# Low parts of the wide groups' weights moved from GpSimd to VectorE, eight PSUM banks in those groups, and two seams reordered

## The chip, the cores and the metric

One core of a Trainium2 chip runs the whole program. The metric is device time of one execution in microseconds (us), the median of the runs; lower is better. TensorE (PE in the rows) runs the matrix multiplies, VectorE (DVE), ScalarE (ACT) and GpSimd (POOL) the elementwise work, and the sync engine's queue (SP) issues most DMAs.

## The reference

A two-layer model steps over 1024 prompt rows, 16 meta rows and 8 x 16 decode rows: an mLSTM layer, then a sliding-window attention layer, each followed by the same kind of feed-forward block. Only the two feed-forward blocks matter here:

```python
def swiglu(x, w_gu, w_dn):
    g, u = jnp.split(x @ w_gu, 2, axis=-1)
    return (jax.nn.silu(g) * u) @ w_dn
...
h = h + swiglu(rmsnorm(h, norm_ffn[l]), w_gate_up[l], w_down[l])
```

`w_gu` is 1024 x 5632 and `w_dn` 2816 x 1024, all float32. The first block runs on 1168 rows of tokens, the second on 1152.

## The kernel before

The class `Ffn` is one feed-forward block; it is used twice. Every float32 operand is split into a high part (ScalarE's copy to the fp32r type, `product_hi`, L415) and a low part (the operand minus its high part, `product_lo`, L426), and a product is three matmuls: high x high, high x low, low x high.

A block has three stages. First four plain column blocks of gate and up (L835 to L848). Then 20 **wide groups** g = 0 to 19: each makes two column blocks of gate (g even) or up (g odd) by Strassen's scheme in Winograd's form, seven products i = 0 to 6 instead of eight. A product (`wide_product`, L723) is 24 matmuls of 292 (second block: 288) columns with four 128-row weight tiles. Products are numbered p = 7g + i. Then 10 **down groups** (g = 20 to 29) do the same for `w_dn` (`down_product`, L750), where a product has two halves nn of 12 matmuls. Below, the **entry** is wide group 0 and what leads to it, and the **down seam** is the step from group 19 to group 20.

Nothing is scheduled by a tool: every engine has its own order, written out by hand, and semaphores between engines. Around a product p these are the steps:

- SP loads four weight quarters of 128 x 512 for each group (`load_quarter`, L308). Quarters A11 and A21 of the next group wait for low parts i = 2 and 3 of this group, A12 for i = 5 and A22 for i = 6.
- Four sums of quarters (`weight_sum` n = 0 to 3, L432) make the weights of products 2 to 5: GpSimd does them for group 0, VectorE for all others (`weight_sums`, L1066).
- ScalarE makes the high part of product p + 2 after product p - 1 is done (L423, L676); GpSimd then makes its low part at once (L492 to L516). Weights sit in a ring of three.
- TensorE waits for the low part of p and for the eviction of p - 2 (L727 to L731); the products alternate between two pairs of PSUM banks.
- VectorE, in order: the eviction of p (`wide_out`, L919), then sums of weights, then forms of the hidden rows (`form_sum`, L976). In an odd group the evictions of products 1, 4 and 5 are three operations in a row: add from PSUM (L950), scale (L953), multiply with the gate (L961).

At the entry VectorE also makes the operands t2, t3 and t4 of the products and their low parts (`t_low`, L900). At the down seam the forms of the hidden rows come back from DRAM (`load_hidden`, L326), ScalarE makes their high parts (L616), and the low parts (`hidden_low`, L467) are VectorE's, but for forms 1 and 3, which are GpSimd's (L496, L501).

Of the kernel before, what the change touches and what calls it, by code (L numbers as in the profile page):

```python
# [139 lines left out]
class Ffn:  # L140


    def __init__(self, nc, a, s, name, layer, gain, parity, base, early, tok, before, turns=None):
# [45 lines left out]
        self.t_raw, self.t_scaled, self.t4_lo = share["t_raw"], share["t_scaled"], share["t4_lo"]  # L189
# [7 lines left out]
        counts = dict(w_hi=4 + 210 + 2, w_lo=8 + 210 + 4, w_sum=4 * 30, x_hi=40, x_lo=38, x_sq=24, x_sum=21, t_raw=16, t_scaled=8,  # L197
                      t4_lo=4, total=3, root=3, rst=3, gu_done=12 + 140 + 140, gu_evac=12 + 140 + 140, silu=46, hid=46,
                      g_scaled=30, u_scaled=30, hid_hi=41, hid_lo=39, hid_sum=40, dn_done=self.n_down, dn_evac=self.n_down)
# [153 lines left out]
    def sync(self, sp, last=None):  # L353
# [10 lines left out]
        for g in range(WIDE_GROUPS + DOWN_GROUPS):  # L364
            for i in range(N_PRODUCTS):
# [49 lines left out]
    def product_hi(self, act, p):  # L415
# [7 lines left out]
        act.wait_ge(self.gu_done, self.done_at(p - 3))  # L423
# [34 lines left out]
    def t_low_pool(self, pool, k):  # L458

        hi, lo = self.wide_x(6, k)  # L460
        if k == 2:
            for x in range(4):
                pool.wait_ge(self.hid_st[x], self.z["hid_st"][x] + 16)
        pool.wait_ge(self.x_hi, self.z["x_hi"] + 36 + k - 1)
        pool.tensor_tensor(lo, self.wide_raw(6, k), hi.bitcast(F32), ALU.subtract).then_inc(self.t4_lo, 1)

    def hidden_low(self, eng, kk, j, done):  # L467

        m = 7 * kk + j
        hi, lo = self.combo(m)  # L470
        eng.wait_ge(self.hid_hi, self.z["hid_hi"] + m + 1)
        eng.tensor_tensor(lo, self.hidden_raw(m), hi.bitcast(F32), ALU.subtract).then_inc(done, 1)

# [12 lines left out]
    def gpsimd(self, pool):  # L486
# [5 lines left out]
        for g in range(WIDE_GROUPS + DOWN_GROUPS):  # L492
            p = 7 * g
            self.product_lo(pool, p)
            if g == WIDE_GROUPS:
                self.hidden_low(pool, 0, 1, self.t4_lo)  # L496
            if g == 0:
# [2747 lines left out]
```

## Time and profile before

| | us |
|---|---|
| median of 3 runs | 2460.42 (2460.22 to 2460.51) |
| the profiled execution | 2460.95 |
| its span, first to last instruction | 2459.2 |
| TensorE busy | 2410.8 (98%) |
| VectorE busy | 1673.7 (68%) |
| GpSimd busy | 990.4 (40%) |
| ScalarE busy | 865.4 (35%) |
| mean granted clock of TensorE | 0.995 |

Busy time is the time in which an engine ran an instruction of the program; idle time of an engine that is not the bottleneck costs nothing. A window of the trace is given from its start to its end in us of the span. PEclk is the share of full speed that TensorE's clock was granted.

### The profile page before, as it was taken

What the parts mean: (1) busy time and instruction counts of PE and PEld (TensorE: products, weight loads), DVE (VectorE), ACT (ScalarE), POOL (GpSimd) and SP (SyncE); (2) the same over time, 40 slices, a digit from 0 to 9 for tenths busy, and PEclk for the clock granted to TensorE, in tenths of its full rate; (3) what the DMA queues carried; (4) which work ended last, traced back from release to release, by engine and by line L of the source; (5) the groups of instructions that cost most, each with busy time, mean ns of one, the idle gap of its engine ahead of it and who ended that gap; (6) DMA issues with size and microseconds to landing.
All of it is one profiled execution on the core that took longest, in us unless ns stands there. A gap on an engine that the chain in (4) does not pass through costs nothing. (4 is left out here: it accounts for less than half of the span.)

```text
span 2459.2 us, 42910 instructions
## 1 busy us (share of the span) xinstructions
PE 2410.8 (98%) x16730; PEld 2340.1 (95%) x16730; DVE 1673.7 (68%) x2540; ACT 865.4 (35%) x1765; POOL 990.4 (40%) x818
## 2 busy tenths in 40 slices
PE   9999999999999999999999999999999999999997
PEld 8989999999999999999999989889999999999996
DVE  6445454439767667697879656757877776788775
ACT  5223232326222222243425556436322222243334
POOL 1222222422544444444447344335544444444542
PEclk9999999999999999999999999999999999999999
DMA  4445565211222223264522234210132332254423
GB/s 160 144 131 146 166 179 181 71 36 38 86 87 98 91 92 101 84 208 141 165 87 59 46 81 104 57 35 27 64 106 72 97 108 90 97 193 148 135 87 122
DMA packets 303533, 259.50 MB, mean 106 GB/s; under 512 B 52856, under 2 KB 261164, under 8 KB 303300
## 3 DMA queue, kind: packets, MB, share of 16 engines
q1 hardware_dynamic: 303140, 256.70, 34.1%
q8 instruction: 135, 2.21, 0.4%
q14 instruction: 66, 0.54, 0.1%
q10 hardware_dynamic: 192, 0.04, 0.0%
HBM read 180.95 MB, written 77.54 MB: 105 GB/s over the span
## 5 line engine op out<-in xcount | busy, mean ns | idle before, releaser
L430 POOL TENSOR_TENSOR wh<-raw,wh 128x512 fp32r<-128x512 f32 x360 | 525.9, 1461 | 645.0 <-ACT wh L424 644.7
L424 ACT ACTIVATE wh<-raw 128x512 fp32r<-128x512 f32 x360 | 227.3, 631 | 700.8 <-PE psum L746 261.4
L746 PE MATMUL psum<-xh,wh 128*128 128x292 f32 (+1 forms) x2560 | 460.3, 296 | 7.1 <-DVE ffn_gate_quarters L941 6.6
L746 PEld LDWEIGHTS psum<-xh,wh 128*128 128x128 f32 x2560 | 383.7, 189 | 7.7 <-issue 7.7
L746 PE MATMUL psum<-xl,wh 128*128 128x292 f32 (+1 forms) x1280 | 276.6, 298 | 0.0
L2781 PE MATMUL psum<-xh,wh 128*128 128x384 f32 (+1 forms) x792 | 274.6, 347 | 1.3 <-DVE fr_tmp L2971 0.5
L2781 PE MATMUL psum<-xl,wh 128*128 128x384 f32 (+1 forms) x792 | 270.0, 341 | 0.0
L2781 PE MATMUL psum<-xh,wl 128*128 128x384 f32 (+1 forms) x792 | 268.8, 339 | 0.0
L974 DVE TENSOR_TENSOR h<-h,psum 128x584 f32<-128x584 f32 (+1 forms) x280 | 205.1, 752 | 83.2 <-PE psum L771 82.9
L771 PE MATMUL psum<-ffn_slot,wh 128*128 128x292 f32 (+1 forms) x1536 | 212.5, 300 | 9.7 <-DVE ffn_part L946 9.7
L771 PEld LDWEIGHTS psum<-ffn_slot,wh 128*128 128x128 f32 x1536 | 210.2, 192 | 10.3 <-issue 10.3
L746 PEld LDWEIGHTS psum<-xl,wh 128*128 128x128 f32 x1280 | 206.4, 189 | 0.0
L2781 PEld LDWEIGHTS psum<-xh,wh 128*128 128x128 f32 x792 | 148.8, 188 | 3.9 <-DVE xl L2941 1.1
L2781 PEld LDWEIGHTS psum<-xh,wl 128*128 128x128 f32 x792 | 149.1, 188 | 0.1
L2781 PEld LDWEIGHTS psum<-xl,wh 128*128 128x128 f32 x792 | 148.9, 188 | 0.1
L2654 POOL TENSOR_TENSOR wl<-raw,wh 128x512 fp32r<-128x512 f32 x62 | 82.6, 1353 | 138.3 <-ACT wh L2467 138.3
L771 PE MATMUL psum<-xh,wh 128*128 128x292 f32 (+1 forms) x960 | 130.9, 296 | 0.0
L771 PEld LDWEIGHTS psum<-xh,wh 128*128 128x128 f32 x960 | 128.7, 188 | 0.0
L430 POOL TENSOR_TENSOR wh<-ffn_w_extra,wh 128x512 fp32r<-128x512 f32 x60 | 84.3, 1406 | 95.4 <-ACT wh L424 95.4
L746 PE MATMUL psum<-ffn_t2h,wh 128*128 128x292 f32 (+1 forms) x640 | 117.6, 295 | 2.8 <-issue 2.8
L746 PE MATMUL psum<-ffn_t1h,wh 128*128 128x292 f32 (+1 forms) x640 | 117.5, 295 | 1.9 <-POOL wh L430 1.9
L771 PE MATMUL psum<-xl,wh 128*128 128x292 f32 (+1 forms) x864 | 118.8, 296 | 0.0
(330 smaller groups left out, 5128.1 us busy)
## 6 DMA issues: line engine op xcount, KB each, us to landing
raw<-in_w_gate_up SPq DMA_DIRECT2D x160, 256.0 KB, 3.5
raw<-in_w_down SPq DMA_DIRECT2D x80, 256.0 KB, 3.1
ffn_form_d<-ffn_gate_quarters SPq DMA_DIRECT2D x50, 292.0 KB, 2.2
ffn_form_d<-ffn_gate_quarters SPq DMA_DIRECT2D x50, 288.0 KB, 2.2
raw<-in_a_w_in SPq DMA_DIRECT2D x24, 512.0 KB, 4.8
ffn_slot_raw<-ffn_form_d SPq DMA_DIRECT2D x16, 584.0 KB, 5.0
fr_qkv<-qkv_d SPq DMA_DIRECT2D x36, 256.0 KB, 3.8
ffn_slot_raw<-ffn_form_d SPq DMA_DIRECT2D x16, 576.0 KB, 5.2
```

The lines of the kernel that those rows point to most:

```text
L424: act.activation(self.ring(p)[0], self.quarter(b), ACT.Copy).then_inc(self.w_hi, 1)
L430: pool.tensor_tensor(lo, self.quarter(WEIGHT_OF[p % 7]), hi.bitcast(F32), ALU.subtract).then_inc(self.w_lo, 1)
L746: y = pe.matmul(psum[:, bank + c, 0:N], w[:, k, :], x[:, N * c:N * c + N], start=(FRESH[i] and k == 0 and m == 0), stop=(k == 3 and m == 2 ...
L771: y = pe.matmul(psum[:, bank + c, 0:N], w[:, k, cols], x[:, k, N * c:N * c + N], start=(FRESH[i] and k == 0 and m == 0), stop=(k == 1 and ...
L974: dve.tensor_tensor(x, x, psum[:, bank:bank + 2, 0:N], ALU.add).then_inc(self.gu_evac, 1)
L2654: pool.tensor_tensor(wl[:, slot_of(n), v], raw[:, n % 2, v], wh[:, slot_of(n), v].bitcast(F32), ALU.subtract).then_inc(w_lo, 1)
L2781: mm_ = pe.matmul(psum[:, g % DB, 0:nt], w[:, k, :], x[:, k, t0:t0 + nt], start=(k == 0 and m == 0), stop=(k == KD - 1 and m == 2))
```

## The change

In the wide groups, low parts of the weights from p = 9 to p = 139 are made by VectorE, right behind the eviction of p - 2; GpSimd keeps p = 0 to 8 and the down groups. The products of even groups use banks 0, 1, 4, 5 and those of odd groups 2, 3, 6, 7, so the first two products of a group wait for no eviction of the group before. At the entry ScalarE makes the high parts of products 0 and 1 earlier, GpSimd does all four sums right after low parts 0 and 1, and two low parts of operand t4 go from GpSimd to VectorE. At the down seam three sums of group 20 go from VectorE to GpSimd, ahead of its low part 141; two hidden low parts go from GpSimd to VectorE; the hidden forms are loaded in another order; and the first down product waits half by half for older evictions.

```diff
+    def wide_bank(self, g, i):
+        return 2 * (g % 2) + 4 * (i % 2)
...
     def sync(self, sp, last=None):
                     if i == 2:
                         self.load_quarter(sp, g + 1, A11)
                         self.load_quarter(sp, g + 1, A21)
+                    if g == 19 and i in (3, 4):
+                        for j in ((0, 1), (2,))[i - 3]:
+                            self.load_hidden(sp, 0, j)
                     if i == 4:
                         self.load_quarter(sp, g + 1, A12)
                     if i == 5:
                         self.load_quarter(sp, g + 1, A22)
-                if g == 19 and i >= 3:
-                    for j in ((0, 1), (2, 3), (4, 5), (6,))[i - 3]:
+                if g == 19 and i >= 5:
+                    for j in ((3,), (4, 5, 6))[i - 5]:
                         self.load_hidden(sp, 0, j)
...
     def product_hi(self, act, p):
-        act.wait_ge(self.gu_done, self.done_at(p - 3))
+        act.wait_ge(self.gu_done, self.done_at(p - 3) if p > 1 else self.z["gu_done"] + 8 + p)
...
     def gpsimd(self, pool):
-        for g in range(WIDE_GROUPS + DOWN_GROUPS):
-            p = 7 * g
+        for p in range(7 * (WIDE_GROUPS + DOWN_GROUPS)):
+            if 9 <= p < 140:
+                continue
+            if p == 140:
+                self.weight_sum(pool, WIDE_GROUPS, 0)
+                pool.wait_ge(self.w_lo, self.lo_at(139))
             self.product_lo(pool, p)
...
+            if p < 2:
+                self.weight_sum(pool, 0, p)
+            if p == 1:
+                self.weight_sum(pool, 0, 2)
+                self.weight_sum(pool, 0, 3)
+            if p == 7 * WIDE_GROUPS:
+                self.weight_sum(pool, WIDE_GROUPS, 1)
+                self.weight_sum(pool, WIDE_GROUPS, 2)
...
     def scalar(self, act, x_free, h_ready):
         gate_part(0)
-        for k in (2, 3, 0, 1):
-            t2_hi(k)
+        t2_hi(2)
+        t2_hi(3)
+        self.product_hi(act, 0)
+        self.product_hi(act, 1)
+        t2_hi(0)
+        t2_hi(1)
         gate_part(1)
         t3_scale(0)
         t3_scale(1)
-        self.product_hi(act, 0)
-        self.product_hi(act, 1)
...
         def wide_product(g, i):
-            bank = 4 * ((g + i) % 2)
+            bank = self.wide_bank(g, i)
             pe.wait_ge(self.w_lo, self.lo_at(p))
             if p < 2:
                 pe.wait_ge(self.gu_evac, self.z["gu_evac"] + (8, 12)[p])
+            elif g == 1 and i < 2:
+                pe.wait_ge(self.root, self.z["root"] + 3)
+            elif i < 2:
+                pe.wait_ge(self.gu_evac, self.evac_at(7 * (g - 2) + 6 - i))
             else:
                 pe.wait_ge(self.gu_evac, self.evac_at(p - 2))
...
         def down_product(g, i):
-                pe.wait_ge(self.gu_evac, self.evac_at(p - 2, nn))
+                if p == 140:
+                    pe.wait_ge(self.gu_evac, self.evac_at(7 * (18 + nn) + 6))
+                else:
+                    pe.wait_ge(self.gu_evac, self.evac_at(p - 2, nn))
...
         def weight_sums(g, i):
-            if i in (4, 5, 6) and g + 1 < WIDE_GROUPS + DOWN_GROUPS:
+            if i in (4, 5, 6) and g + 1 < WIDE_GROUPS + DOWN_GROUPS and g + 1 != WIDE_GROUPS:
                 self.weight_sum(dve, g + 1, i - 4)
...
                 wide_out(g, i)
...
+                if 9 <= 7 * g + i + 2 < 140:
+                    if 7 * g + i + 2 == 9:
+                        dve.wait_ge(self.w_lo, self.lo_at(8))
+                    self.product_lo(dve, 7 * g + i + 2)
                 weight_sums(g, i)
...
+                if g == 0 and i == 2:
+                    for x in range(4):
+                        dve.wait_ge(self.hid_st[x], self.z["hid_st"][x] + 16)
+                    t_low(6, 2, 37)
+                    t_low(6, 3, 38)
...
                 if g == 19 and i in (4, 6):
-                    hidden_lo(0, i // 2 - 2 if i == 4 else 2)
+                    for j in ((0, 1), (), (2,))[i - 4]:
+                        hidden_lo(0, j)
...
                 down_out(g, i)
                 weight_sums(g, i)
+                if g == WIDE_GROUPS and i == 0:
+                    hidden_lo(0, 3)
```

## Rows read from the trace of the kernel before

**Rows 1.** The page, part 1: busy us (share of the span) xinstructions.

```profile
PE 2410.8 (98%) x16730; PEld 2340.1 (95%) x16730; DVE 1673.7 (68%) x2540; ACT 865.4 (35%) x1765; POOL 990.4 (40%) x818
```

**Rows 2.** Windows: us; busy of PE, PEld, DVE, ACT, POOL (instructions); PEclk; DMA share; GB/s.

```profile
600.43:631.69 31.26, 24.97 (x170) 24.12 (x169) 30.36 (x28) 12.09 (x20) 19.34 (x13) 0.95 0.15 46
721.90:1015.09 293.19, 293.19 (x2186) 293.19 (x2185) 206.33 (x233) 73.57 (x117) 125.60 (x91) 1.00 0.29 92
1060.20:1090.54 30.34, 25.42 (x170) 25.21 (x169) 30.27 (x28) 14.28 (x16) 17.04 (x10) 0.89 0.77 252
1731.62:1761.43 29.81, 24.31 (x169) 23.67 (x169) 28.97 (x28) 12.39 (x20) 18.03 (x12) 0.94 0.16 48
1805.86:2139.06 333.20, 333.20 (x2523) 333.20 (x2522) 235.52 (x269) 84.93 (x134) 151.12 (x105) 1.00 0.29 94
2183.67:2213.38 29.71, 24.97 (x168) 24.76 (x169) 29.64 (x28) 14.16 (x16) 16.82 (x10) 0.89 0.77 260
```

**Rows 3.** Waits of TensorE: who waited for whom, us in total, times, longest.

```profile
PE psum L746 <- DVE ffn_gate_quarters L941: 6.6, 2, 3.3
PE psum L746 <- POOL wh L430: 1.9, 2, 0.9
```

**Rows 4.** Windows inside the first entry, columns as in rows 2.

```profile
606.80:610.20 3.40, 1.84 (x14) 1.64 (x13) 3.40 (x3) 0.00 (x0) 2.87 (x2) 1.00 0.00 0
617.20:620.20 3.00, 0.00 (x0) 0.00 (x0) 3.00 (x3) 0.69 (x1) 3.00 (x3) 1.00 0.45 135
620.40:623.60 3.20, 3.08 (x13) 3.11 (x14) 3.20 (x4) 1.21 (x2) 3.06 (x3) 0.50 0.03 7
```

**Rows 5.** Timeline of VectorE, wide group 9: start us, us, engine line op.

```profile
828.43 0.77 DVE L950 TENSOR_TENSOR ffn_part<-psum,ffn_part 128x584 f32<-128x584 f32 x1 [2.46 <-PE psum L746]
829.23 1.89 DVE L953 TENSOR_TENSOR ffn_part<-ffn_part,rstd 128x584 f32<-128x584 f32 x1
831.15 0.77 DVE L961 TENSOR_TENSOR ffn_gate_quarters<-ffn_gate_quarters,ffn_part 128x584 f32<-128x584 f32 x1
831.84 0.69 DVE L443 TENSOR_TENSOR ffn_w_extra<-raw 128x512 f32<-128x512 f32 x1
```

**Rows 6.** Timeline of GpSimd, wide group 9.

```profile
829.20 1.30 POOL L430 TENSOR_TENSOR wh<-raw,wh 128x512 fp32r<-128x512 f32 x1 [1.95 <-ACT wh L424]
```

**Rows 7.** The page, part 6: DMA issues xcount, KB each, us to landing.

```profile
raw<-in_w_gate_up SPq DMA_DIRECT2D x160, 256.0 KB, 3.5
```

**Rows 8.** Timeline of VectorE, first entry.

```profile
592.05 1.44 DVE L903 TENSOR_TENSOR ffn_t2l<-ffn_t_raw,ffn_t2h 128x584 fp32r<-128x584 f32 x2
...
612.42 3.63 DVE L903 TENSOR_TENSOR xl<-ffn_part,xh 128x584 fp32r<-128x584 f32 x2
...
619.66 1.43 DVE L941 COPY ffn_gate_quarters<-psum 128x584 f32<-128x584 f32 x2
```

**Rows 9.** Windows of VectorE alone: us, busy, clock, DMA share, GB/s.

```profile
592.00:620.40 28.40, 28.26 (x30) 1.00 0.15 53
1054.00:1106.00 52.00, 51.83 (x53) 0.93 0.65 217
```

**Rows 10.** Window of GpSimd alone, first entry.

```profile
592.00:620.40 28.40, 18.40 (x11) 1.00 0.15 53
```

**Rows 11.** Timeline of TensorE, first down seam.

```profile
1068.56 12.51 PE L771 MATMUL psum<-ffn_slot,wh 128*128 128x292 f32 x72 [4.92 <-DVE ffn_part L946]
```

**Rows 12.** Timeline of VectorE, first down seam.

```profile
1053.96 0.77 DVE L950 TENSOR_TENSOR ffn_part<-psum,ffn_part 128x584 f32<-128x584 f32 x1 [2.46 <-PE psum L746]
...
1057.97 1.37 DVE L472 TENSOR_TENSOR ffn_slot<-ffn_slot_raw,ffn_slot 128x1168 fp32r<-128x1168 f32 x1
...
1067.66 0.75 DVE L946 TENSOR_TENSOR ffn_part<-psum,rstd 128x584 f32<-128x584 f32 x1
...
1105.13 1.42 DVE L974 TENSOR_TENSOR h<-h,psum 128x584 f32<-128x584 f32 x2
```

**Rows 13.** Timeline of ScalarE, first down seam.

```profile
1058.33 1.19 ACT L616 ACTIVATE ffn_slot<-ffn_slot_raw 128x1168 fp32r<-128x1168 f32 x1 [0.65 <-DMA ffn_slot_raw<-ffn_form_d]
```

More of the change, by code:

```diff
@@ L456, in weight_sum @@
         x.then_inc(self.w_sum, 1)
[L458 to L472, printed above, removed]
     def last_lo(self, eng, j, half):
@@ L598, in t4_hi @@
             if k < 2:
-                act.wait_ge(self.t4_lo, self.z["t4_lo"] + k + 1)
+                act.wait_ge(self.x_lo, self.z["x_lo"] + 36 + k + 1)
             act.activation(self.wide_x(6, k)[0], self.wide_raw(6, k), ACT.Copy).then_inc(self.x_hi, 1)
@@ L738, in wide_product @@
             if g == 0 and i == 6:
-                pe.wait_ge(self.t4_lo, self.z["t4_lo"] + 2)
-                pe.wait_ge(self.x_lo, self.z["x_lo"] + 38)
+                pe.wait_ge(self.x_lo, self.z["x_lo"] + 40)
             hi, lo = (w.rearrange("p (k n) -> p k n", k=4) for w in self.ring(p))
@@ L755, in down_product @@
             if sub == 0:
-                if kk == 0 and i in (1, 3):
-                    pe.wait_ge(self.t4_lo, self.z["t4_lo"] + (3 if i == 1 else 4))
-                elif kk == 0:
-                    pe.wait_ge(self.hid_lo, self.z["hid_lo"] + (1, 1, 2, 2, 3, 4, 5)[i])
-                else:
-                    pe.wait_ge(self.hid_lo, self.z["hid_lo"] + 7 * kk + i - 1)
+                pe.wait_ge(self.hid_lo, self.z["hid_lo"] + 7 * kk + i + 1)
             hi, lo = (w.rearrange("p (k n) -> p k n", k=2) for w in self.ring(p))
@@ L792, in down_blocks @@
                 if t % 3 == 0:
-                    pe.wait_ge(self.hid_lo, self.z["hid_lo"] + 33 + 2 * (t // 3 + 1))
+                    pe.wait_ge(self.hid_lo, self.z["hid_lo"] + 35 + 2 * (t // 3 + 1))
                 if t < 2:
@@ L818, in down @@
             for c, (t0, nt) in enumerate(tok):
-                pe.wait_ge(self.hid_lo, self.z["hid_lo"] + 33 + 2 * (c + 1))
+                pe.wait_ge(self.hid_lo, self.z["hid_lo"] + 35 + 2 * (c + 1))
                 for m in range(KD):
@@ L922, in wide_out @@
             pair, up = g // 2 + 1, g % 2
-            bank = 4 * ((g + i) % 2)
+            bank = self.wide_bank(g, i)
             x = psum[:, bank:bank + 2, 0:N]
@@ L996, in hidden_lo @@
         def hidden_lo(kk, j):
-            self.hidden_low(dve, kk, j, self.hid_lo)
+            m = 7 * kk + j
+            hi, lo = self.combo(m)
+            dve.wait_ge(self.hid_hi, self.z["hid_hi"] + m + 1)
+            dve.tensor_tensor(lo, self.hidden_raw(m), hi.bitcast(F32), ALU.subtract).then_inc(self.hid_lo, 1)
         def last_hidden_lo(c):
@@ L2236, in front @@
     started = {x: [0, 0] if x == "w_loaded" else 0 for x in s["share"]}
-    again = dict(w_sum=(ncd, HA), t4_lo=(nco, HA), t_raw=(den, 10 * HA), t_scaled=(hsd, 10 * HA), g_scaled=(ssq, 10 * HA),
+    again = dict(w_sum=(ncd, HA), t_raw=(den, 10 * HA), t_scaled=(hsd, 10 * HA), g_scaled=(ssq, 10 * HA),
                  u_scaled=(msd, 10 * HA), hid_sum=(rden, 10 * HA))
```

30 lines of the change are left out of this document (4 added, 26 removed).

## The prediction

> **What bounds the kernel now.** I read the busy shares first: TensorE is busy 98% of the span [rows 1], so all idle time of it together is 48 us. Then I looked where that time lies, with windows cut at the starts of groups [rows 2]. In the stretch 721.90 to 1015.09 of the first block (13 wide groups, 91 products) TensorE is busy 293.19 of 293.19 us, one product each 3.222 us; in the second block 333.20 of 333.20 us for 105 products, 3.173 each. Nothing waits there, so faster low parts and more banks have nothing to gain in those groups. The time is lost at four seams: the entries last 31.26 and 29.81 us against 22.55 and 22.21 for a steady group, the first down groups, with as many matmuls, 30.34 and 29.71 [rows 2]. That is 8.7 + 7.6 + 7.8 + 7.5 = 31.6 us, the ceiling of any gain.
>
> The waits of TensorE say who ends these losses: VectorE's evictions L941 and the low parts of GpSimd [rows 3]; at the first down seam 4.92 us for the eviction L946 [rows 11]. Part of the loss is the clock. In the entry TensorE did nothing from 617.20 to 620.20, and the granted clock was then 0.5, that is 1.2 GHz, from 620.40 to 623.60 while it was busy; a stop of about 1.5 us at 606.80 to 610.20 left it at 1.0, that is 2.4 GHz [rows 4]. Last I asked why VectorE is late, and the answer is that it is saturated: 28.26 of 28.40 us before the entry's worst stop, and 51.83 of 52.00 us across the down seam [rows 9].
>
> **How VectorE and GpSimd meet.** Two low parts of 128 x 584 take 1.44 us on VectorE alone and 3.63 us beside a busy GpSimd; two evictions of the same size from PSUM take 1.43 us, GpSimd busy or not [rows 8]. So an operation with both inputs in SBUF that meets one of GpSimd pays (3.63 - 1.44) / 2 = 1.1 us, and one that reads PSUM pays nothing. In wide group 9 the scaling L953 took 1.89 us while GpSimd's low part ran at 829.20; the multiply after it, of the same shape, 0.77 us [rows 5, 6].
>
> **Part 1, the low parts on VectorE in the wide groups.** Without GpSimd there, no operation of VectorE pays the 1.1 us. But the low part now stands in VectorE's order, behind the eviction. I lay out the second half of an odd group with free durations [rows 5]: add, scale and multiply start 0.80 us apart, and the low part 0.69 after the multiply, so 2.29 us from the first start; it takes 0.69 (the sum L443 has its size and its two SBUF inputs) and ends at 2.98. The sum behind product 4 starts at 2.89, and product 5's chain at 3.49, since back-to-back operations overlap by 0.09; its low part, which product 0 of the next group needs, ends at 3.49 + 2.98 = 6.47. Group 9 starts at 721.90 + 4 x 22.553 = 812.11, its product 5 at 828.22, the next group at 834.66. VectorE starts on product 4 at 828.43, so the low part ends at 834.90. From the end of an eviction, 1067.66 + 0.75, to TensorE's start at 1068.56 are 0.15 us [rows 11, 12]; I take 0.1 of them as the signal. TensorE starts 0.34 us late. Behind product 1 of an odd group the low part ends 0.21 + 2.98 + 0.1 = 3.29 us after a product's start, 0.07 late. Even groups have two operations at most and recover. Nine of the ten odd groups precede a wide group: 9 x 0.34 + 10 x 0.07 = 3.8 us. In the second block two periods are 0.10 us shorter and VectorE's operations some 0.07: 9 x 0.37 + 10 x 0.08 = 4.1. **Toll: +8 us.** Bounds: 5 us if the signal costs nothing, 20 if each of the three long evictions of an odd group stops TensorE by 0.35.
>
> What else hangs on this order: quarter A22 of the next group is issued once low part i = 6 is made, now behind the eviction of product 4 instead of about 4 us earlier on GpSimd. Its sum is wanted behind product 5, at 6.38 us in the layout above; 2.98 + 3.5 us [rows 7] is 6.48, so VectorE may stand 0.1 us there. Behind that stand the eviction of product 6 and low part 1 of the next group, which has 0.5 us to spare. I cost it at nothing; a load 0.6 us slower than the median would show. A12 is issued one eviction earlier and lands in time. The banks are costed at nothing too: no eviction ends a wait in the steady stretch, neither before nor in this layout.
>
> **Part 2, the entry.** VectorE stays the bound, so I count what it meets up to the eviction that releases product 4 (619.66 before, [rows 8]). Its list of operations up to there is the same; the two t4 low parts come behind it. Before, GpSimd runs eleven operations from 592 to 620.4 [rows 10], the last of them, a t4 low part, at its end; of the ten others about one falls beside PSUM reads, so they cost it some 9.8 us. Now high parts 0 and 1 come some 3 us earlier, as soon as their quarters land, and low parts 0 and 1 and all four sums run in one train of six from about 592 to 602.5, each against an operation with two SBUF inputs; low parts 2 to 5 meet four more. Ten meetings are 11 us, and where VectorE reaches an operation just after GpSimd has begun it pays up to 1.2: 11.3. So product 4 starts 1.5 us later than at 620.5. The waits move forward: product 1 now waits some 3 us for the last up eviction (L881), 2 about 1.9, 3 about 0.8, 4 about 2.5. Against that, the 3.08 us of matmuls at 1.2 GHz [rows 4] cost 1.5 us before, and with shorter stops I take the clock as full. Net 0 in the first block, +0.4 in the second, where VectorE had been idle ahead of the train. Bounds for each block: -4.4 (four meetings fewer) to +3 (the clock falls again, and one meeting more).
>
> **Part 3, the down seam.** VectorE begins at 1053.96 [rows 12]. Three eviction operations and low part 139 end at 1056.95. GpSimd's low part 140 waits for that and holds VectorE to 1058.2; two hidden low parts of 1.28 us each (row at 1057.97, less the overlap) follow to 1060.75, their high parts being there by 1059.5 [rows 13, 12]. Product 138's chain, with two meetings with GpSimd's sums, ends at 1064.6, and the eviction of 139 at 1065.4, where it was 1068.41. TensorE's product 140 starts at 1060.2, but its second half now waits for that eviction: 3.6 us. Product 141 then starts at 1067.1 instead of 1068.56. VectorE goes on with hidden low parts 2, 3 and 4 and two evictions; product 143 waits 1.5 us for the eviction of 141 at 1074.9. That is 5.2 us lost for 7.8 before, **-2.6 us**, and -2.4 in the second block.
> Why not more: VectorE has no pause up to 1106 [rows 9]. Its addition for product 150 (first half) ends at 1105.88 [rows 12], and product 152, which needs it, starts at 1090.54 + 5 x 3.222 = 1106.65: a slack of 0.8. What TensorE wins earlier it gives back there, but for what VectorE itself wins: about 2 us, as it makes 0.6 + 2.6 us more, three sums of 0.6 less, and meets GpSimd for some 6 us instead of 9.4. Bounds: -7.8 (seam gone) to +3 for each block.
> On SP the hidden forms 0 to 2 go ahead of A12, which now waits for low part 138; A12 lands about 1 us later, covered by GpSimd's two sums ahead of low part 141.
>
> **Sum.** 2460.95 (the profiled execution: span 2459.2 and 1.75 around it) + 8 + 0.4 - 5.0 = 2464.35. That execution is 0.53 above the median, so **2464**. A measurement of this kernel can tell 0.2%, 4.9 us: the band of no change is 2455.5 to 2465.3. My own range for this case, 2459 to 2470, crosses its upper end. Chance 0.54, of which 0.34 inside the band and 0.20 above.
>
> The steady toll is a short stop of TensorE about every 22 us, a stop of 0.3 us, and a stop of 1.5 us left the clock at 2.4 GHz [rows 4]. The Trainium skill, page "TensorE: Matmul & The Clock Gate", section "A second HAM failure mode: psum-queue depth-cycling", speaks against this change: it says that small idle gaps between groups of matmuls can by themselves make the clock swing between its two levels. By that rule the sum would be the fourth rival below.
>
> **The rivals.**
> *Slower, by the seam.* The hidden low parts 0 and 1 now stand ahead of two evictions on VectorE, and wait for forms that come over DMA. For it: DMA engines are busy 0.77 of the first down group [rows 2], and ScalarE waited for the second form until 1058.33 [rows 13]. Each us by which its high part comes after 1059.5 goes through to the eviction of 139. If it comes as late as 1061.7, product 141 starts at 1069.2, the clock falls as before, and the seam costs 0.6 us more than before instead of 2.5 less: +6.2 for both, 2471. Against it: the first three forms are issued earlier than before. It decides from about 1061 on. Chance 0.18.
> *Faster, VectorE freed.* If GpSimd's early train meets PSUM reads and pauses, four meetings fewer give -4.4 us at each entry, and the seams another 1.5: 2464 - 8.8 - 3 = 2452. For it: the train comes before VectorE's longest run of SBUF operations. Against it: VectorE has no pause from 592 on [rows 9], and only some six of its operations up to product 4 read PSUM. Chance 0.22.
> *No toll.* The change may not lengthen VectorE's order as I lay it out, if the long evictions run shorter than their free rows: 2456. Against it: 0.77 us stands in every such row. Chance 0.04.
> *Clock.* If each of the 20 odd groups' stops brings 3.2 us at half speed, 1.6 us lost each [rows 4], 32 us are added: 2496. Against it are the stop of 1.5 us that left the clock alone [rows 4] and the clock of 1.0 in the steady stretches, where nothing stops [rows 2]. Chance 0.02.
>
> **How the numbers follow.** Faster 0.22; the same 0.34 + 0.04 = 0.38; slower 0.20 + 0.18 + 0.02 = 0.40. The range goes from 2452, the faster case, to 2475, above the seam's case and with a toll of some 16 us: outside lie half of the faster case, the clock and a tail, under 0.2.
>
> **What would show it.** Right: in the odd groups TensorE waits some 0.3 us for VectorE's L430 at the start of the next group, and VectorE's L953 takes 0.77 everywhere; the entries stay near 31 us with the longest waits on L881, L941; product 140 stops between its halves. Wrong: no idle TensorE in wide groups 1 to 19 (no toll), entries of 27 us or less, a down seam under 24 us, or a granted clock of 0.5 inside the steady stretch.

## The result, and the profile after

The changed kernel takes **2466.76 us** (median of 9 runs, 2464.96 to 2469.66); the kernel before, beside it on the same chip, 2460.22 (9 runs, 2459.48 to 2463.93). The ratio is 1.0027 with a 95% interval of 1.0019 to 1.0035: slower by 6.5 us. 2464 was forecast, with a range of 2452 to 2475. The profiled execution of after has a span of 2464.2 us, 5.0 longer than the one before.

The page, part 1, of after (busy us, share of the span, instructions), which answers to [rows 1]:

```profile
PE 2416.2 (98%) x16730; PEld 2337.1 (95%) x16730; DVE 1714.0 (70%) x2804; ACT 869.8 (35%) x1765; POOL 611.2 (25%) x554
```

GpSimd has lost 379 us of work, and VectorE has gained only 40, though it makes 262 of the low parts: most of what they cost it saves on meetings.

Windows of after, cut at the starts of its groups as [rows 2] (columns as there): in each block the entry, the wide groups 1 to 19, the first and the second down group.

```profile
600.65:630.43 29.78, 25.07 (x170) 24.22 (x169) 29.38 (x33) 12.08 (x20) 13.05 (x9) 0.94 0.16 49
630.43:1063.63 433.20, 433.19 (x3194) 429.54 (x3193) 321.99 (x470) 112.33 (x173) 2.59 (x2) 1.00 0.30 96
1063.63:1091.17 27.54, 23.01 (x170) 22.57 (x169) 26.75 (x27) 14.07 (x17) 15.31 (x10) 1.00 0.78 262
1091.17:1117.24 26.07, 23.33 (x170) 22.65 (x169) 24.11 (x28) 7.95 (x11) 11.50 (x8) 1.00 0.41 134
1735.37:1764.60 29.23, 23.16 (x169) 22.32 (x169) 28.84 (x34) 11.95 (x20) 10.82 (x7) 1.00 0.18 57
1764.60:2191.22 426.62, 426.54 (x3195) 422.64 (x3193) 319.75 (x470) 112.10 (x173) 2.63 (x2) 1.00 0.30 96
2191.22:2218.83 27.61, 23.97 (x171) 23.74 (x169) 27.51 (x29) 14.22 (x17) 14.29 (x10) 0.94 0.80 271
2218.83:2241.02 22.19, 22.19 (x171) 22.19 (x170) 19.98 (x27) 7.60 (x10) 10.61 (x7) 1.00 0.46 148
```

From the same cuts in both traces: the wide groups took 428.51 and 422.24 us before, so they lose 4.7 and 4.4. The entries win 1.5 and 0.6, the first down groups 2.8 and 2.1. The second down group of the first block, 22.49 before, now takes 26.07 and gives 3.6 back. With 0.7 won elsewhere that is the 5.0 of the spans.

PE counts as busy in nearly the whole wide stretch, and its list of waits has nothing there. The weight loads (PEld) have lost 3.7 and 4.0 us of it (429.54 of 433.20, 422.64 of 426.62; before, 428.50 of 428.51 and 422.01 of 422.24), and their own list of waits names VectorE's low part L436, 18 times:

```profile
PEld psum L731 <- DVE wh L436: 4.2, 18, 0.2
```

How it comes about shows where VectorE's list is laid beside the start of the next group (timelines of VectorE and of TensorE, wide group 9 of after, columns as in [rows 5]):

```profile
832.76 0.76 DVE L933 TENSOR_TENSOR ffn_part<-psum,ffn_part 128x584 f32<-128x584 f32 x1
833.55 0.77 DVE L936 TENSOR_TENSOR ffn_part<-ffn_part,rstd 128x584 f32<-128x584 f32 x1
834.35 0.77 DVE L944 TENSOR_TENSOR ffn_gate_quarters<-ffn_gate_quarters,ffn_part 128x584 f32<-128x584 f32 x1
835.04 0.68 DVE L436 TENSOR_TENSOR wh<-raw,wh 128x512 fp32r<-128x512 f32 x1
```

```profile
835.36 0.43 PE L731 MATMUL psum<-ffn_t4h,wh 128*128 128x292 f32 x2
835.78 0.54 PE L731 MATMUL psum<-xh,wh 128*128 128x292 f32 x2
```

Matmuls start every 0.134 us, so the next pair was due at 835.63; the low part (L436) ends at 835.72 and TensorE goes on at 835.78, a stop of 0.15 us. The first pair behind it takes 0.54 us instead of 0.43, another 0.11. This second price is also paid where TensorE does not stop at all. At product 3 of the odd group the low part ends at 822.47, in time for the matmul due at 822.52. But elsewhere the load of a matmul's weights starts 0.13 us ahead of it, during the matmul before, and here load and matmul start together (loads and matmuls at product 3, of after, then of lo_ahead, an experiment below in which no product of these groups waits):

```profile
822.52 0.19 PEld L731 LDWEIGHTS psum<-ffn_t1h,wh 128*128 128x128 f32 x1
822.52 0.40 PE L731 MATMUL psum<-ffn_t1h,wh 128*128 128x292 f32 x1
```

```profile
820.47 0.19 PEld L731 LDWEIGHTS psum<-ffn_t1h,wh 128*128 128x128 f32 x1
820.60 0.29 PE L731 MATMUL psum<-ffn_t1h,wh 128*128 128x292 f32 x1
```

The trace of before shows this price as well, behind a stop in its first entry:

```profile
613.70 0.54 PE L746 MATMUL psum<-ffn_t1h,wh 128*128 128x292 f32 x2 [0.93 <-POOL wh L430]
614.07 0.43 PE L746 MATMUL psum<-ffn_t1l,wh 128*128 128x292 f32 x2
```

In after it is paid at product 6 too (832.30, its low part ready at 832.24). So a pair of groups loses 0.48 us: 0.11 in product 3 (3.32 us instead of 3.22), 0.11 in product 6 and the stop of 0.15 behind it (3.48 together), and 0.11 in product 0 of the next group (3.34). In each block that is nine stops, 1.3 and 1.5 us in all, and 29 such starts, 3.1 us. Where 0.26 us is called a stop in the expectations below, that is the 0.11 of product 6 and the stop of 0.15 behind it. L953 (L936 in after), which took 1.89 us before [rows 5], takes 0.77.

Waits of TensorE in after, in place of [rows 3]:

```profile
PE psum L754 <- DVE ffn_part L929: 7.2, 2, 3.6
PE psum L731 <- DVE ffn_gate_quarters L924: 4.2, 2, 2.1
PE psum L731 <- DVE ffn_up L864: 3.8, 2, 2.0
PE psum L754 <- DVE h L957: 3.7, 4, 1.6
```

The first is the stop between the halves of product 140: only the first half of it waits for an older eviction than before (132), the second for a newer one (139; in the kernel before it was 138). The next two are products 4 and 1 of the entries. Of the last, three are new, in the second down group of the first block; the fourth, 0.9 us, is product 143.

### The profile page after: what moved, and what is told of

Read it like the earlier page. It is cut to its first block and busy times, and to the rows that moved or that the text cites. A ratio compares the mean times of both kernels' runs of the same rounds, so it can differ in the third digit from the quotient of the medians.

```text
span 2464.2 us, 42912 instructions
## 1 busy us (share of the span) xinstructions
PE 2416.2 (98%) x16730; PEld 2337.1 (95%) x16730; DVE 1714.0 (70%) x2804; ACT 869.8 (35%) x1765; POOL 611.2 (25%) x554
## 5 line engine op out<-in xcount | busy, mean ns | idle before, releaser
L731 PE MATMUL psum<-xl,wh 128*128 128x292 f32 (+1 forms) x1280 | 276.0, 297 | 0.0
L436 POOL TENSOR_TENSOR wh<-raw,wh 128x512 fp32r<-128x512 f32 x136 | 208.4, 1534 | 242.8 <-ACT wh L430 235.3
L449 POOL TENSOR_TENSOR ffn_w_extra<-raw 128x512 f32<-128x512 f32 x4 | 6.1, 1523 | 845.0 <-DMA raw<-in_w_down 845.0
L436 DVE TENSOR_TENSOR wh<-raw,wh 128x512 fp32r<-128x512 f32 x224 | 152.8, 682 | 0.0
L731 PE MATMUL psum<-ffn_t4h,wh 128*128 128x292 f32 (+1 forms) x640 | 120.1, 299 | 0.0
```

The costliest lines, as they stand in the source:

```text
L436: pool.tensor_tensor(lo, self.quarter(WEIGHT_OF[p % 7]), hi.bitcast(F32), ALU.subtract).then_inc(self.w_lo, 1)
L449: x = pool.tensor_tensor(q(EXTRA), q(A11), q(A21), ALU.subtract)
L731: y = pe.matmul(psum[:, bank + c, 0:N], w[:, k, :], x[:, N * c:N * c + N], start=(FRESH[i] and k == 0 and m == 0), stop=(k == 3 and m == 2 ...
```

## The experiments

The table has the medians, the ratio to before with its interval, and the stages of each profiled execution, cut at the starts of groups as above (us; first block / second block). The kernels ran on several chips; each ratio is to before on the same chip, and there before took 2460.0 to 2460.5.

| kernel | median | ratio (95%) | entry | wide 1-19 | 1st down group | 2nd down group |
|---|---|---|---|---|---|---|
| before | 2460.22 | 1 | 31.26 / 29.81 | 428.51 / 422.24 | 30.34 / 29.71 | 22.49 / 22.18 |
| after | 2466.76 | 1.0027 (1.0019-1.0035) | 29.78 / 29.23 | 433.20 / 426.62 | 27.54 / 27.61 | 26.07 / 22.19 |
| lo_gpsimd | 2457.99 | 0.9993 (0.9984-1.0002) | 29.78 / 30.75 | 428.52 / 422.05 | 26.47 / 26.85 | 22.49 / 22.18 |
| lo_only | 2470.70 | 1.0047 (1.0034-1.0060) | 31.35 / 29.92 | 433.78 / 427.48 | 29.92 / 28.54 | 22.49 / 22.19 |
| old_banks | 2467.13 | 1.0030 (1.0019-1.0042) | 30.37 / 30.74 | 434.46 / 428.06 | 26.00 / 25.38 | 22.69 / 26.03 |
| lo_ahead | 2453.84 | 0.9978 (0.9969-0.9987) | 29.77 / 31.17 | 428.51 / 422.05 | 26.67 / 26.23 | 22.49 / 24.76 |
| before_lo_ahead | 2460.22 | 1.0000 (0.9991-1.0009) | 31.37 / 28.47 | 428.51 / 424.39 | 28.80 / 26.29 | 25.04 / 24.75 |
| seam_undone | 2473.89 | 1.0057 (1.0045-1.0070) | 31.30 / 30.72 | 433.47 / 427.34 | 31.55 / 30.84 | 22.49 / 22.18 |
| entry_undone | 2465.20 | 1.0024 (1.0015-1.0033) | 32.30 / 30.02 | 433.31 / 427.64 | 28.85 / 26.47 | 22.49 / 26.16 |
| sums_late | 2454.07 | 0.9977 (0.9968-0.9986) | 31.91 / 30.63 | 428.51 / 422.05 | 26.83 / 28.01 | 22.49 / 22.19 |
| seam_form_later | 2453.19 | 0.9973 (0.9963-0.9983) | 29.76 / 30.75 | 428.51 / 422.05 | 27.00 / 26.67 | 22.49 / 22.19 |
| best_old_entry | 2454.61 | 0.9977 (0.9968-0.9986) | 31.38 / 29.96 | 428.51 / 422.05 | 26.95 / 26.68 | 22.49 / 22.19 |
| entry_vector | 2443.81 | 0.9933 (0.9920-0.9945) | 25.87 / 24.87 | 428.51 / 422.05 | 27.30 / 26.63 | 22.49 / 22.19 |
| low141_first | 2444.55 | 0.9935 (0.9921-0.9949) | 25.87 / 24.81 | 428.51 / 422.05 | 27.04 / 27.90 | 22.65 / 22.19 |

### Where the toll comes from: lo_gpsimd, lo_only, old_banks, lo_ahead, before_lo_ahead

**lo_gpsimd**: the changed kernel, low parts back on GpSimd.

```diff
-            if 9 <= p < 140:
-                continue
...
-                pool.wait_ge(self.w_lo, self.lo_at(139))
...
-                if 9 <= 7 * g + i + 2 < 140:
-                    if 7 * g + i + 2 == 9:
-                        dve.wait_ge(self.w_lo, self.lo_at(8))
-                    self.product_lo(dve, 7 * g + i + 2)
```

> The changed kernel, with the low parts of the wide groups back on GpSimd; the eight banks, the entry and the down seam stay as changed. Theory (the toll is the place of the low parts in VectorE's order): the 0.26 us stop ahead of the product that follows each odd group, and the two slow restarts with it, go; wide groups 1 to 19 take 428.5 and 422.2 us again instead of 433.2 and 426.6, 9.1 us less, and the time is near 2457.5 us if entry and seam stay as they are. Rival 1 (the toll is the eight banks, whose owners are waited for): nothing changes, 2466. Rival 2 (what VectorE is spared beside an idle GpSimd pays at the down seam): the toll goes, but the low parts 133 to 139 meet VectorE's work there, and up to 3 us per block come back, 2459 to 2463.

2457.99 us, 8.8 less than after, and the wide groups are back at 428.52 and 422.05. Banks, entry and seam were left in, so the toll is the low parts' alone. (The profiled execution, at 2452.77, is the lowest of eleven; the steady wide groups are the safest thing to read in it.) Rival 2 is not seen: the first down groups are not longer than after's, and the median is that of the theory. The kernel is also all of the change but its main part, and is 2.1 us below the 2460.08 of before beside it, with an interval that does not exclude no change at all.

**lo_only**: the kernel before, with the lines that lo_gpsimd takes out put in, and nothing else.

> The kernel before, with only the low parts 9 to 139 of the wide groups moved to VectorE; four banks at a time, entry and down seam as before. Theory (place in VectorE's order): the toll alone, 9 us, and at the seams nothing or a little, 2467 to 2471 us; TensorE stops some 0.26 us behind each odd group. Rival 1 (the banks cause the toll): 2460, no stop. Rival 2 (freeing VectorE of GpSimd is worth more than the toll at the seam): 2464.

2470.70 us, at the upper end of the theory: the toll without the gains.

**old_banks**: the changed kernel, with

```diff
-        return 2 * (g % 2) + 4 * (i % 2)
+        return 4 * ((g + i) % 2)
...
-            elif i < 2:
-                pe.wait_ge(self.gu_evac, self.evac_at(7 * (g - 2) + 6 - i))
...
-                if p == 140:
-                    pe.wait_ge(self.gu_evac, self.evac_at(7 * (18 + nn) + 6))
-                else:
-                    pe.wait_ge(self.gu_evac, self.evac_at(p - 2, nn))
+                pe.wait_ge(self.gu_evac, self.evac_at(p - 2, nn))
```

> The changed kernel with the bank pairs of the kernel before: two pairs in turn, and each product waits for the eviction of the second one before it. Theory: the banks cost and gain nothing in the wide groups, so 2465 to 2468 us with the same stop of 0.26 us behind the odd groups; at the down seam the first half of product 140 then waits for the eviction of 138 and no longer for that of 139 between its halves. Rival (the eight banks cause the toll): 2457.5. Second rival (the banks hide a part of the toll): 2470 or more, with longer stops in the odd groups.

2467.13 us, the same as after. The longer wide stretch (by 1.3 and 1.4) is mostly the wait for the eviction of 138, which now comes ahead of product 140; the first down groups are shorter by 1.5 and 2.2. No effect of the eight banks on the time could be measured.

**lo_ahead**: the changed kernel with the same operations in another order.

```diff
         for i in range(N_PRODUCTS):
+            if 9 <= 7 * g + i + 2 < 140:
+                if 7 * g + i + 2 == 9:
+                    dve.wait_ge(self.w_lo, self.lo_at(8))
+                self.product_lo(dve, 7 * g + i + 2)
             wide_out(g, i)
...
-            if 9 <= 7 * g + i + 2 < 140:
-                if 7 * g + i + 2 == 9:
-                    dve.wait_ge(self.w_lo, self.lo_at(8))
-                self.product_lo(dve, 7 * g + i + 2)
             weight_sums(g, i)
```

> The changed kernel with one edit: VectorE makes the low part of product p + 2 ahead of its evicting operations for product p instead of behind them. All operations stay, only their order on VectorE changes. Theory (place in the order): VectorE is busy some 34 of 45 us in a pair of wide groups, so it has room; the low part is then made one product earlier, no product waits for it, wide groups 1 to 19 take 428.5 and 422.2 us and the time is near 2457.5 us, or below if the earlier quarter loads help the down seam. Rival 1 (VectorE has too much to do in an odd group, whatever the order): the stop stays or moves to an eviction, 2464 to 2468. Rival 2 (the eight banks): 2466.

2453.84 us: 12.9 less than after, and faster than before. Windows of the wide stretches, and the timeline of VectorE in the same odd group:

```profile
630.49:1059.00 428.51, 428.51 (x3194) 428.51 (x3193) 322.47 (x471) 112.88 (x174) 3.51 (x3) 1.00 0.30 98
1757.53:2179.58 422.05, 422.05 (x3194) 422.05 (x3193) 320.24 (x471) 112.49 (x173) 4.21 (x3) 1.00 0.31 99
```

```profile
829.52 0.69 DVE L449 TENSOR_TENSOR ffn_w_extra<-raw 128x512 f32<-128x512 f32 x1
830.12 0.68 DVE L436 TENSOR_TENSOR wh<-raw,wh 128x512 fp32r<-128x512 f32 x1
830.73 0.76 DVE L933 TENSOR_TENSOR ffn_part<-psum,ffn_part 128x584 f32<-128x584 f32 x1
```

The low part now stands ahead of the chain of its product (L933, L936, L944), is made 3.0 us earlier against the group's start (19.2 us into it, where after has 22.2), and nothing waits for it. VectorE's work is the same 322 us in the stretch: it was the place, not the amount. In the profiled executions, whose spans differ by 10.0 us, the wide groups give 9.3 and the first down groups 2.3: product 140 stops 2.3 us between its halves instead of 3.6.

**before_lo_ahead**: the kernel before, with low parts on VectorE in this order.

> The kernel before with only the low parts 9 to 139 moved to VectorE, each ahead of the evicting operations instead of behind them; banks, entry and down seam as before. Theory (the low parts ahead cost nothing and by themselves gain nothing in the wide groups, where nothing waited): no stop in the wide groups, 428.5 and 422.2 us; the first down groups 29 to 30 and 28 to 29 us; 2458 to 2460.5 us. Rival (a VectorE without GpSimd beside it reaches the down seam earlier and needs no reordered seam): first down groups under 27 us, 2454.

2460.22 us, the kernel before to within the interval. Well placed, the low parts on VectorE cost nothing and gain nothing. Its first down groups are shorter (28.80, 26.29), but both second ones give 2.6 back, and the end of the second wide stretch loses 2.3.

### The seam: seam_undone, sums_late, seam_form_later

**seam_undone**: the changed kernel with the parts of the diff at groups 19 and 20 taken back (sums on VectorE, hidden low parts 1 and 3 on GpSimd, SP's old order).

> The changed kernel with the down seam of the kernel before: VectorE makes the sums of the first down group, GpSimd the hidden low parts 1 and 3, and SP issues the hidden forms in the old order; low parts on VectorE, eight banks and the entry stay as changed. Theory (the seam as changed takes about 5 us off the two first down groups, and gives up to 3.6 us back in the second down group of a block): the first down groups take about 29.9 and 28.6 us, as in the run with the low parts alone on VectorE, instead of 27.5 and 27.6, and the second ones 22.5 and 22.2, so the time is 2466.5 to 2470 us. Rival (the seam won nothing that stays): 2464 to 2466.5.

2473.89 us, 7.1 more than after and beyond the theory. First down groups 31.55 and 30.84: the seam is worth 4.0 + 3.2 there, less the 3.6 that it gives back later. The waits of TensorE say why it is worse than lo_only's: with eight banks the second half of product 140 waits for the eviction of 139 (6.6 us), where in lo_only both halves ran before that wait (4.6 us, ahead of product 141).

```profile
PE psum L763 <- DVE ffn_part L938: 13.1, 2, 6.6
```

In this execution the entries, which it left alone, are 1.5 us longer each than in that of after; that is most of the rest. In both of these entries the granted clock fell behind product 4.

**sums_late**: lo_ahead, with the last pair's form sums and their stores in group 23.

```diff
-                if g == WIDE_GROUPS + 1 and i < 4:
+                if g == WIDE_GROUPS + 3 and i < 4:
                     form_sum(10, i)
```

It was made for the second down group. There, in after, the timeline of VectorE reads:

```profile
1091.97 0.69 DVE L454 TENSOR_TENSOR raw<-raw,ffn_w_extra 128x512 f32<-128x512 f32 x1 [1.49 <-DMA raw<-in_w_down]
...
1099.73 1.85 DVE L966 TENSOR_TENSOR ffn_part<-ffn_gate_quarters 128x584 f32<-128x584 f32 x1
...
1104.74 1.85 DVE L970 TENSOR_TENSOR ffn_part<-ffn_gate_quarters,ffn_part 128x584 f32<-128x584 f32 x1
```

A quarter lands 1.49 us late, VectorE's list slips, and two form sums of 0.75 meet GpSimd's low parts at 1.85.

> The kernel with the low parts made ahead of the evictions (lo_ahead), with one further edit: the four form sums of the last pair, which VectorE makes in the second down group, come two groups later, with their stores. Nobody needs them before the last chunk. Theory (the second down group stops because VectorE has no slack there and these sums meet GpSimd's low parts, 1.85 us for 0.75, once a late quarter shifts its list): the stops of some 2.6 us in the second down group are gone in both blocks, the median is 0 to 2.6 us below lo_ahead's 2453.8, near 2452.5, and the runs spread less upward. Rival (the stops come from the late quarter itself): the second down group still loses 1 to 3 us where it did, 2453.8. Rival 2 (the spread of the runs is that of the clock at the seams): the spread stays.

The loss is gone: 22.49 and 22.19, and no kernel with this edit takes more than 22.65, while of the six with the reordered seam or the low parts ahead, but without it, five lose 2.6 to 4.0 in a block or in both. But the time is 2454.07, that of lo_ahead, and the runs spread as widely (2452.24 to 2458.03): Rival 2.

**seam_form_later**: sums_late, and

```diff
-                    for j in ((0, 1), (), (2,))[i - 4]:
+                    for j in ((0,), (), (1, 2))[i - 4]:
                         hidden_lo(0, j)
```

> As sums_late, and one further edit: VectorE makes hidden low part 1 behind the eviction of product 139 instead of ahead of that of 138. Theory (the second half of product 140 waits for the eviction of 139, behind two hidden low parts of 1.3 us): the stop between the halves of product 140 falls from 2.3 to about 1.0 us, and the first down groups take 1 us less each, some 2450.5 us. Rival (product 141 then waits for hidden low part 1 in its place, since VectorE is saturated): the stop moves by one product, and the time is that of sums_late, near 2452.5. Rival 2 (shorter stops keep the clock up): another 1.7 us less for each seam at which the granted clock no longer falls.

2453.19 us. The stop between the halves of 140 falls to 0.6 us, and product 141 waits 1.6, product 143 1.5; the first down groups take 27.00 and 26.67, after 26.83 and 28.01. The stop moved, as the rival had it.

### The entry: entry_undone, best_old_entry, entry_vector

**entry_undone**: the changed kernel with ScalarE's order, the four sums and the t4 low parts of the entry as before.

> The changed kernel with the entry of the kernel before: high parts 0 and 1 behind the scalings, each sum of the first wide group behind a low part, and the two t4 low parts on GpSimd; low parts on VectorE, eight banks and the down seam stay as changed. Theory (the entry as changed gains 1.5 and 0.6 us): the entries take about 31.3 and 29.9 us instead of 29.8 and 29.2, and the time is near 2469 us. Rival 1 (as forecast, the entry is worth nothing): 2466 to 2467. Rival 2 (the changed entry costs elsewhere, as its train of GpSimd holds VectorE): 2465 or less.

2465.20 us, 1.6 less than after. **best_old_entry** takes the same edit back from seam_form_later:

> As seam_form_later, with the entry of the kernel before. Theory (as forecast, the changed entry is worth nothing by itself, and how long an entry is depends on whether the granted clock falls in it): the same time within 1.5 us of seam_form_later's 2453.2; the entries take about 31.3 and 29.9 us. Rival (the changed entry gains 2.1 us, as the profiled execution of the changed kernel alone suggests): 2455.3 or more.

2454.61 us, 1.4 more. Two tests of opposite sign, whose intervals overlap: by itself the reordered entry wins or loses nothing that could be measured, to some 2 us. Where the 2.1 us of the two profiles come from shows when the entries are cut at the first matmul of product 4 (columns as in [rows 2]; four windows of before, then four of after):

```profile
600.43:620.52 20.09, 13.80 (x98) 12.95 (x97) 20.02 (x20) 8.73 (x14) 13.37 (x9) 0.99 0.14 44
620.52:631.69 11.17, 11.17 (x73) 11.17 (x73) 10.34 (x9) 3.35 (x6) 5.97 (x5) 0.86 0.17 48
1731.62:1750.50 18.88, 13.38 (x98) 12.74 (x97) 18.81 (x20) 8.66 (x14) 11.49 (x8) 0.99 0.15 46
1750.50:1761.43 10.93, 10.93 (x72) 10.93 (x73) 10.15 (x9) 3.73 (x6) 6.54 (x5) 0.86 0.17 50
```

```profile
600.65:620.69 20.04, 15.34 (x98) 14.48 (x97) 19.94 (x23) 7.93 (x13) 8.17 (x6) 0.91 0.19 58
620.69:630.43 9.74, 9.74 (x73) 9.74 (x73) 9.44 (x11) 4.15 (x7) 4.88 (x3) 1.00 0.11 30
1735.37:1755.01 19.64, 13.57 (x97) 12.73 (x97) 19.54 (x24) 7.87 (x13) 5.98 (x4) 1.00 0.21 68
1755.01:1764.60 9.59, 9.59 (x72) 9.59 (x73) 9.30 (x11) 4.08 (x7) 4.84 (x3) 1.00 0.12 35
```

Up to product 4 VectorE is the bound, and the change wins nothing there: 20.04 us for 20.09, and 19.64 for 18.88. Behind it the length is the clock's: 9.7 and 9.6 us where it stayed up, 11.2 and 10.9 where it fell. The clock fell in the first entry of after too, but behind product 1, and that costs nothing, as TensorE has to wait for VectorE at product 4 anyway: in the second block product 4 starts 19.6 us into the entry whether the clock fell behind product 1 (seam_undone, seam_form_later) or not (after, lo_gpsimd, sums_late). Windows of TensorE alone (us; busy; clock), first two of after, behind products 1 and 4, then two of sums_late, which has the same entry, around the start of product 4:

```profile
606.50:609.80 3.30, 3.30 (x16) 0.50 0.16 60
620.80:624.00 3.20, 3.20 (x25) 1.00 0.02 5
```

```profile
620.00:621.90 1.90, 0.34 (x2) 1.00 0.47 133
622.00:625.40 3.40, 3.40 (x16) 0.50 0.01 2
```

Behind a stop of 1.99 us after went on at 1.2 GHz, behind one of 2.09 us at 2.4 GHz; behind one of 2.11 us sums_late went on at 1.2 GHz, 16 matmuls in 3.40 us for 25 in 3.20. Over all executions in the table the changed entry takes 30.4 and 30.6 us on average (seven kernels), the old one 31.5 and 29.6 (five); behind product 4 the clock fell in 8 of 14 changed entries and in 9 of 10 old ones.

**entry_vector**: seam_form_later, with GpSimd's nine low parts and four sums of the entry made by VectorE too.

```diff
+        self.product_lo(dve, 0)
+        self.product_lo(dve, 1)
         take(self.up, 1, 0, 3, 10)
         product(1, 0, 10)
+        self.weight_sum(dve, 0, 0)
+        self.weight_sum(dve, 0, 1)
...
                 if g == 0 and i == 0:
                     for k in (2, 3):
                         t3_raw(k)
+                    self.weight_sum(dve, 0, 2)
+                    self.weight_sum(dve, 0, 3)
+                if g == 0 and i in (1, 2, 4, 5):
+                    self.product_lo(dve, (3, 5, 7, 8)[(1, 2, 4, 5).index(i)])
...
-            if 9 <= p < 140:
+            if p < 140:
                 continue
```

> As seam_form_later, with GpSimd out of the entry too: VectorE makes the low parts 0 to 8 and the four sums of the first wide group. Theory (what VectorE pays in the entry are its meetings with GpSimd): up to the release of product 4 ten meetings cost it 9.7 us; making those ten operations itself costs 10 x 0.61 = 6.1 us, so product 4 is released some 3 us earlier, the entries take about 27 us instead of 29.8 and 30.7, and the time is 2446 to 2449 us. Rival (the new operations wait in VectorE's order for ScalarE's high parts, and hold up what stands behind them): the stops move to other products, the entries stay at 29 to 32 us, 2452 to 2456.

**2443.81 us** (2443.58 to 2444.26), 16.6 less than before: it beats both kernels. Timelines of VectorE in the first entry, of seam_form_later and then of entry_vector, at the low parts that product 4 needs (L886, there L881):

```profile
614.23 3.62 DVE L886 TENSOR_TENSOR xl<-ffn_part,xh 128x584 fp32r<-128x584 f32 x2
617.77 2.52 DVE L886 TENSOR_TENSOR xl<-ffn_xl_raw,xh 128x584 fp32r<-128x584 f32 x2
```

```profile
612.95 1.44 DVE L881 TENSOR_TENSOR xl<-ffn_part,xh 128x584 fp32r<-128x584 f32 x2
614.31 0.76 DVE L881 TENSOR_TENSOR xl<-ffn_xl_raw,xh 128x584 fp32r<-128x584 f32 x1
614.98 0.69 DVE L436 TENSOR_TENSOR wh<-ffn_w_extra,wh 128x512 fp32r<-128x512 f32 x1
615.59 0.76 DVE L881 TENSOR_TENSOR xl<-ffn_xl_raw,xh 128x584 fp32r<-128x584 f32 x1
```

The last of them ends 3.9 us earlier, though VectorE has made nine operations more by then. Windows of the two entries:

```profile
601.00:626.87 25.87, 23.33 (x169) 22.68 (x169) 25.70 (x39) 12.50 (x20) 0.00 (x0) 1.00 0.18 56
1723.65:1748.52 24.87, 22.93 (x170) 22.33 (x170) 24.70 (x38) 12.41 (x20) 0.00 (x0) 1.00 0.19 60
```

3.9 and 5.9 us less than seam_form_later, and the clock stays at 1.00. Product 4 starts 3.9 and 4.4 us earlier in the entry; the other 1.5 us of the second are the clock's, which fell behind product 4 there in seam_form_later. The longest stop left in an entry is 1.4 us. The five runs lie within 0.7 us; but low141_first, with the same entry, spreads over 4.6, so the narrow spread is not shown to be the entry's.

**low141_first**: entry_vector, with GpSimd's low part 141 ahead of its second and third sum, and hidden low part 1 one place earlier on VectorE.

> As entry_vector, with the order at the down seam changed once more: GpSimd makes low part 141 ahead of its second and third sum, and VectorE makes hidden low part 1 behind the eviction chain of product 138 instead of behind that of 139. Theory (in entry_vector product 141 starts 3 us late, since GpSimd's low part 141 stands behind two sums that meet VectorE and a late quarter): low part 141 is made 4 us earlier; the second half of product 140 then waits about 1 us for the eviction of 139 and product 141 starts some 2 us earlier; the first down groups take 25 to 25.5 us instead of 27.3 and 26.6, and the time is 2441 us. Rival (VectorE is saturated at the seam, so what is won at product 141 is lost again at 142 or 143): first down groups near 26.5 us, 2443 to 2444.

2444.55 us, no gain. VectorE at the seam:

```profile
1055.11 2.47 DVE L979 TENSOR_TENSOR ffn_slot<-ffn_slot_raw,ffn_slot 128x1168 fp32r<-128x1168 f32 x1
1057.51 0.75 DVE L924 TENSOR_TENSOR ffn_part<-psum,rstd 128x584 f32<-128x584 f32 x1
```

Hidden low part 1 met GpSimd (2.47 us for the 1.36 that it takes alone), and the eviction of 139 behind it came at 1058.26: the stop of 2.9 us at product 141 has become one of 2.0 us at product 140 in this block, with 1.9 instead of 1.3 at product 143, and one of 3.9 at product 140 in the second. What is won at one product is lost at another, as the rival had it. Whether a down seam with no GpSimd in it gains as the entry did was not tried.

## Why the prediction was right

The sum was 2464.35; the median is 2466.76, and the sign was right, though the chance for slower was only 0.40. Part of the nearness is luck: in the profiled executions, where 3.4 us were forecast and 5.0 came, the toll came out 1.1 us above its term, the entry 2.5 below, the seam 3.7 above and the rest 0.7 below nothing, and these errors cancel to 1.6. By its steps:

- **The toll** was put at 8 us, 0.34 and 0.07 at two places in each odd group. It is 9.1 in the profile, and 10.5 by the medians of lo_only and before. The place was right, and so was VectorE's list: from the first operation for product 4 to the low part behind product 5 are 6.45 us, where 6.47 were laid out. What it costs TensorE was taken apart wrongly: it waits only 0.15 us, once in a pair of groups, and the load of the first weights, which a low part that is just in time no longer lets run ahead, costs 0.11 at three places. That is 6.2 of the 9.1 us, and the prediction has no term for it, though the trace of before shows the price in its entry (0.54 us for the two matmuls at 613.70, 0.43 for the next two). That 8 stands so near 9.1 is in part luck. lo_ahead and lo_gpsimd remove the toll, old_banks does not. The bounds, 5 and 20, held it.
- **What else hangs on the order** was costed at nothing, and VectorE stood 0.1 us at the late quarter sum (835.85 behind 835.72). That no scaling pays for GpSimd any more was right, and worth nothing in the wide groups, as before_lo_ahead shows.
- **The entry** was put at +0.4: product 4 released 1.5 us later, and the clock full behind it. By the two profiles the entries won 2.1; the two tests put them within some 2 us of zero. Product 4 starts 0.05 us earlier in the first block and 0.8 later in the second. Ten meetings there were in the first, as counted, but at 9.7 us and not 11.3: eight of 1.1, and two of 0.5 with a smaller operation (L872). The clock was full behind product 4 in both entries of this execution, but fell there in 8 of the 14 entries with this order, so that half of the step held here by chance. The waits came earlier, as said, and were shorter: 2.0 for L864, where 3 were forecast.
- **The down seam** was put at -5.0, and in the profile this term is mis-sized most. The stop between the halves of 140 was forecast at 3.6 us and is 3.59; product 143 waits 0.9, where 1.5 was forecast; the first down groups win 4.9. But the give-back in the second down group, for which a slack of 0.8 us at product 152 was allowed and 2 us of VectorE's own savings counted against it, was 3.6 us in one block: a quarter 1.49 us late and two form sums that met GpSimd. Net -1.3 in the profile. sums_late takes the loss out of the trace, but no change in the time could be measured for it. By the medians everything but the low parts is worth 3.9 us (lo_only less after), where 4.6 were forecast for entry and seam; so how far the seam's term was off over many executions stays open.
- **The rivals.** Slower by the seam: it needed a seam 0.6 us longer than before in all, and the first down groups came out 2.8 and 2.1 shorter; the 3.6 us were lost a group later, for another reason. VectorE freed: the entries did not shorten for that reason; four meetings fewer were not to be had by moving GpSimd's work, but, as entry_vector shows, by giving all of it to VectorE. No toll: refuted, though by its letter the sign that was named for it came true, as PE was busy for 433.19 of 433.20 us. Clock: in the wide stretches the granted clock stayed at 1.00 with a stop of 0.15 us in every second group. The rule of the Trainium skill's page "TensorE: Matmul & The Clock Gate", section "A second HAM failure mode: psum-queue depth-cycling", on small idle gaps between groups of matmuls, is not borne out for gaps as short and rare as these.

The Trainium skill's page "SBUF — State Buffer", section "Who interferes with whom", says that a VectorE instruction with two SBUF inputs contends with a GpSimd instruction that reads SBUF. The runs agree: 1.85 us against 0.76 for 128 x 584, and a reader of PSUM is unharmed (L924 takes 0.75 in low141_first at 1057.51, beside an operation of GpSimd, as it does alone).

## What to carry to other kernels

Work that is moved onto an in-order engine is paid for by its place in the order, not by the engine's busy share: ask what it stands behind, and whether its inputs are there early enough to put it ahead. Weights that are ready just in time for their matmul are late already: here their load, begun with the matmul instead of 0.13 us ahead of it, cost 0.11 us each time. Where two engines hold each other up, doing the small operation on the busy engine (0.61 us) can be cheaper than the meeting (1.1 us), most of all where that engine is the bound. And a stage whose length depends on whether the clock falls can't be judged from one execution on each side: take the same stage from all kernels that share it, or undo the edit.

## What was not expected

- 9 us were lost in stretches in which PE counts as busy nearly throughout and its list of waits has nothing. They show in the row of the weight loads, and in starts that come 3.48 us apart instead of 3.22.
- A stop of some 2 us in the entry was followed by the full clock in one place and by half of it in another, even in the same execution; the stop of 3.6 us at the down seam of after was followed by 1.00 in the first block and by a fall in the second (0.94 over the group). What decides stays open. In the four entries of entry_vector and low141_first, whose longest stop is 1.4 us, the clock did not fall.
- Meetings cost GpSimd as well: two of its low parts, 1.3 us each alone, take 4.79 us beside the hidden low parts at the seam of entry_vector (timeline of GpSimd):

```profile
1059.24 4.79 POOL L436 TENSOR_TENSOR wh<-raw,wh 128x512 fp32r<-128x512 f32 x2
```
